# Gate and up products of a feed-forward layer: a second Strassen level for one of seven products, and a first tile whose loads are issued by need

## Chip, core and metric

One core of a Trainium2 chip runs the whole program. The metric is the device time in microseconds (us) of one execution; lower is better. The engines named below are TensorE (PE, with PEld for its weight loads), VectorE (DVE), ScalarE (ACT), GpSimd (POOL) and SyncE (SP), whose queue issues most of the DMAs.

## What is computed

One step of a hybrid layer over 1024 prompt rows and 32 sample rows of width 1024, all in fp32. An input projection feeds two groups of heads, attention and a recurrent mixing; their outputs are concatenated, projected and added to the input. The last part, where most of the change lies, is the feed-forward layer:

```
def layer_tail(x, attn, rw, attn_out_g, w_out, norm_ffn_g, w_gate, w_up, w_down):
    mix = jnp.concatenate([rmsnorm(attn, attn_out_g), rw], axis=-1)
    h = x + mix @ w_out
    u = rmsnorm(h, norm_ffn_g)
    return h + (jax.nn.silu(u @ w_gate) * (u @ w_up)) @ w_down
```

`w_gate` and `w_up` are 1024 x 2816, `w_down` is 2816 x 1024, and `u` has 1056 rows.

## The kernel before

The program has three stages. `layer_inputs` (L265 on) runs the input projection and the recurrence over nine tiles of 128 rows; `prompt_attention` follows, and `tail` (L2422 on) does the output projection and the feed-forward layer. Every engine has its own list of instructions in the order in which it is written; they meet at semaphores, so the order of the work is the written one.

**First tile of `layer_inputs`.** SP issues, in this order, the first tile `xt[0]`, the constants `gmix` and `con`, three of the six pieces of `w_in` (slots `wsl[0..2]`, 1472 KB each), a fourth piece in `area`, the second tile `xt[1]`, the vectors `vec`, and, after two pieces are done (`p_ok` 2), three smaller weights (L371 to L377). POOL waits for the constants, squares `xt[0]` and then multiplies it by `gmix` (L1526, L1528). PE makes six pieces; for pieces 4 and 5 ACT reloads slots 0 and 1 on its own DMA queue as soon as it has copied out the piece that used the slot, and slot 2 for the next tile (L1230).

**Gate and up in `tail`.** With FH = 11, KH = 4 and NW = 264, a *unit* is one pair of output blocks of 128 columns of `w_gate` or `w_up` (22 units), and each unit has two *steps*, one for each half `nh` of the columns of `u` (44 steps). A step is one level of Strassen-Winograd: seven products in place of eight, each of KH = 4 matmuls of 128x128 by 128x264, in four PSUM banks X, Y, Z, W. PE's order in a step is X = A11 B11 (copied out by ACT as `p1_`), Y = S2 T2, Z = S3 B12, W = S1 T1, then the three that close a bank: X += A12 B21, Z += A22 T4, W += S4 B22. `S1..S4` are sums of weight blocks that POOL makes for each unit (L2809 to L2814), `T1, T2, T4` sums of `u` that DVE makes once. DVE makes `u2 = Y + p1` (L2924), `u3 = Z + u2` (L2926) and `u3 = W + u3` (L2928); PE waits for the second before it closes Z and for the third before it closes W, and for `p1` before it closes X. Steps alternate between two sets of four banks, so that DVE and ACT have the next step's time to scale (by `rb`), gate (`th`, a tanh) and store in `hid`. The weights have two buffers `wA`, one for gate and one for up; a unit's two halves of 512 KB are loaded when the unit that used the buffer last is done.

**Down.** Eight steps of seven products of 11 matmuls on `hid`, with sums of `w_down` by POOL and of `hid` by DVE.

## Time and profile before

| what | value |
|---|---|
| three runs | 1798.8, 1803.51 and 1803.69 us, median 1803.51 |
| the profiled execution, its own time | 1797.16 us |
| its span (first to last instruction) | 1795.4 us |
| PE busy | 1725.1 us, 96% of the span |
| DVE, ACT, POOL busy | 950.4, 413.8 and 616.9 us |
| mean granted TensorE clock | 0.994 |

The profiled execution is one run of the same program with a recorder on. Its own time is 1.8 us above its span and 6.35 us below the median of the three runs, so sums of durations from the trace are made against 1797.16 and then set against the median. fp32 matmuls appear as two records each.

### The profile page before, as it was taken

Reading aid. Unit: us, or ns where it says so; the run is one execution under the profiler, and the core shown is the slowest. Engines: PE = TensorE matmul, PEld = TensorE weight load, DVE = VectorE, ACT = ScalarE, POOL = GpSimd, SP = SyncE. Lnnn points to the kernel's source line nnn. Section 1 sums busy time; section 2 is a strip of 40 time slices with the busy share of each in tenths; the row PEclk is TensorE's granted clock in tenths of the full one; section 3 lists DMA queues with packets and bytes.
Section 4 is the critical chain, followed back from the end, with each engine's and each line's share of the span. In section 5 each row is a group of like instructions: output and inputs, shape, how many; then the busy total and the mean of one; then the engine's idle time right before and its main releaser. Section 6 shows DMA issues by size and latency. Waiting matters only on the chain.

```text
span 1795.4 us, 34819 instructions
## 1 busy us (share of the span) xinstructions
PE 1725.1 (96%) x14732; PEld 1307.8 (73%) x14732; DVE 950.4 (53%) x1759; ACT 413.8 (23%) x945; POOL 616.9 (34%) x431
## 2 busy tenths in 40 slices
PE   5999999999998996999999999999999999999999
PEld 3566666666665664666667888888888888888887
DVE  2857767767767675666436433444434444526322
ACT  2343343343334232555212100011110010000000
POOL 2654653663653552001150221222212221635432
PEclk9999999999999998999999999999999999999999
DMA  8443253243244312620152111011110112333431
GB/s 349 166 154 105 69 166 109 66 159 109 80 134 115 107 38 73 185 60 1 34 208 97 47 48 47 24 47 47 48 48 24 48 47 77 121 105 105 145 96 62
DMA packets 89008, 169.36 MB, mean 94 GB/s; under 512 B 29627, under 2 KB 62987, under 8 KB 84630
## 3 DMA queue, kind: packets, MB, share of 16 engines
q1 hardware_dynamic: 80326, 119.16, 20.8%
q10 hardware_dynamic: 8528, 47.98, 7.7%
q8 instruction: 118, 1.93, 0.4%
q14 instruction: 36, 0.29, 0.0%
HBM read 136.40 MB, written 23.04 MB: 89 GB/s over the span
## 4 chain that ended last, share of the span: by engine, by line
PE 49%; DVE 1%; issue 0%; POOL 0%; ACT 0%; DVEq 0%
PE psum L2627 45%; PE psum L2580 4%; DVE u_sum L2890 0%; DVE mixT L2891 0%; PE psum L2615 0%; POOL row_ms L2804 0%; DVE mixT L2864 0%; DVE hid L2861 0%; DVE rb L2910 0%; PE psum L2621 0%; DVE hid L2851 0%; DVE part L2960 0%; DVE part L2924 0%; DVE yout L3018 0%; DVE part L2926 0%
## 5 line engine op out<-in xcount | busy, mean ns | idle before, releaser
L2627 PE MATMUL psum<-mixT,wA 128*128 128x264 f32 x1408 | 335.2, 386 | 0.4 <-DVE mixT L2891 0.4
L2627 PEld LDWEIGHTS psum<-mixT,wA 128*128 128x128 f32 x1408 | 267.4, 190 | 46.4 <-issue 0.8
L2627 PE MATMUL psum<-u_sum,wA 128*128 128x264 f32 x1232 | 297.2, 386 | 2.3 <-DVE part L2926 1.5
L518 PE MATMUL psum<-wsl,xt 128*128 128x368 f32 (+2 forms) x1100 | 287.7, 452 | 9.4 <-DMA wsl<-in_w_in 6.1
L2627 PEld LDWEIGHTS psum<-u_sum,wA 128*128 128x128 f32 x1232 | 233.8, 190 | 43.0 <-issue 3.2
L518 PEld LDWEIGHTS psum<-wsl,xt 128*128 128x128 f32 (+1 forms) x1100 | 151.9, 172 | 93.8 <-issue 20.0
L2809 POOL TENSOR_TENSOR wA<-wA 128x512 f32<-128x512 f32 x22 | 29.5, 1342 | 392.5 <-DMA wA<-in_w_gate 197.0
L2627 PE MATMUL psum<-hid,wA 128*128 128x264 f32 x528 | 120.2, 386 | 2.1 <-DVE hid L2962 1.5
L2627 PEld LDWEIGHTS psum<-hid,wA 128*128 128x128 f32 x528 | 100.2, 190 | 19.9 <-issue 2.8
L2213 PE MATMUL psum<-kT,qT 104*128 104x346 f32 (+7 forms) x224 | 78.3, 468 | 11.7 <-DMA kT<-scratch_kT 8.3
L1551 POOL TENSOR_TENSOR Ls<-Lraw,con 128x512 f32<-128x512 f32 x45 | 48.7, 1090 | 94.6 <-ACT Lraw L1165 66.1
L2627 PE MATMUL psum<-mixT,u_sum 128*128 128x264 f32 x352 | 79.8, 386 | 0.0
L2771 ACT ACTIVATE p<-psum 128x264 f32<-128x264 f32 x44 | 17.1, 390 | 253.6 <-PE psum L2627 253.4
L2627 PEld LDWEIGHTS psum<-mixT,u_sum 128*128 128x128 f32 x352 | 66.8, 190 | 11.7 <-POOL u_sum L2829 0.4
L1517 POOL TENSOR_TENSOR st<-st,con 128x3 f32<-128x3 f32 (+1 forms) x18 | 50.7, 2815 | 60.7 <-DVE st L1714 31.3
L1165 ACT ACTIVATE proj<-psum,rstd 128x368 f32<-128x368 f32 (+1 forms) x72 | 36.9, 512 | 143.4 <-PE psum L518 142.8
L2301 ACT ACTIVATE pq<-psum,neg 128x346 f32<-128x346 f32 (+7 forms) x112 | 59.8, 542 | 27.1 <-DVE neg L2382 20.9
L2379 DVE TENSOR_REDUCE part<-psum 128x1 f32<-128x347 f32 (+5 forms) x88 | 44.3, 524 | 40.6 <-PE psum L2213 39.5
L2819 POOL TENSOR_TENSOR wA<-wA 128x1408 f32<-128x1408 f32 x8 | 25.3, 3164 | 109.1 <-DMA wA<-in_w_down 109.1
L2790 ACT ACTIVATE p<-psum 128x264 f32<-128x264 f32 x8 | 3.1, 391 | 255.1 <-PE psum L2627 255.1
L2924 DVE TENSOR_TENSOR part<-psum,p 128x264 f32<-128x264 f32 x44 | 19.0, 433 | 79.1 <-PE psum L2627 79.0
L2353 POOL COPY wide<-rec 128x256 f32<-128x256 f32 x16 | 6.4, 400 | 152.0 <-DVE rec L2392 152.0
(367 smaller groups left out, 2898.2 us busy)
## 6 DMA issues: line engine op xcount, KB each, us to landing
wsl<-in_w_in ACTq DMA_DIRECT2D x27, 1472.0 KB, 6.5
wA<-in_w_down SPq DMA_DIRECT2D x32, 704.0 KB, 4.1
wA<-in_w_gate SPq DMA_DIRECT2D x22, 512.0 KB, 4.3
wA<-in_w_up SPq DMA_DIRECT2D x22, 512.0 KB, 4.3
mixed<-proj SPq DMA_DIRECT2D x8, 784.0 KB
...
wsl<-in_w_in SPq DMA_DIRECT2D x3, 1472.0 KB, 13.9
...
```

What stands on the lines that cost most here:

```text
L518: return pe.matmul(out, lhsT, rhs, start=start, stop=stop)
L1165: copy = lambda out, in_, **k: act.activation(out, in_, ACT.Copy, **k)
L1517: tt(out, ms, c_("minus_half")[:, 0:n], ALU.pow).then_inc(s[ok], 1)
L1551: tt(Ls[i % 2][:, :, :], Lraw[:, :, :], bcast(c_("levels")[:, i * 64:(i + 1) * 64], 1, H), ALU.mult).then_inc(s["Ls_ok"], 1)
L2213: pe.matmul(pb[n % BANKS][:, 0:y - x], qT[b][0:ROWS, t * P:(t + 1) * P], kT[b][0:ROWS, x:y], start=True, stop=True).then_inc(s["s_ps"], 1)
L2301: act.activation(rows_of(a, t)[:, x:y], pb[n % BANKS][:, 0:y - x], ACT.Exp, bias=neg[:, i % RINGS:i % RINGS + 1], accum_out=sums[:, pair % ...
L2379: dve.tensor_reduce(part[:, r, u:u + 1], src, AX.X, ALU.max).then_inc(s["part_ok"], 1)
L2580: last = pe.matmul(pb[bank][:, 0:c.stop - c.start], w[:, k, :], g.mixT[:, first_k + k, c], start=start and k == 0, stop=stop and k == 3, s ...
L2627: ins = pe.matmul(pb[bank][:, 0:NW], left(k), right(k), start=first and k == 0, stop=k == depth - 1, skip_group_check=not first)
L2809: tt(S1, A21, A22, ALU.add).then_inc(s["s1_ok"], 1)
L2819: tt(Ahi[:, 0:FH], Alo[:, 0:FH], Ahi[:, 0:FH], ALU.subtract).then_inc(s["e3_ok"], 1)
L2924: named(tt(u2, Y, p1_[it % 2][:, :], ALU.add), "y_done", it + 1)
```

## The change

In the first tile `xt[0]` is squared without a wait for the constants (the multiplication by `gmix` still waits for them), `vec` and the smaller weights are issued only when two pieces are done and slot 0 is reloaded, and slot 2 is reloaded later, after `lora_in(0)`.

In gate and up two units form a *double* (11 doubles: one that mixes gate and up, then five times two gate units and two up units). The product A12 B21 is left out of the four ordinary steps of a double, whose closing of X is gone with it; `p1_` has five buffers, so that the four X products stay. A fifth step makes the four A12 B21 blocks of the double together by a second Strassen level, with DK = 2 matmuls for each of seven products, from the sums `d1..d4` (POOL, for each double) and `t1, t2, t4` (DVE, once). DVE folds the kept products into it. A double of gate stores these corner blocks unscaled and they are scaled and gated in the first step of the next double (`scale_corner`, `gate_corner`). The load of A12 is a DMA of its own, after the fifth step. Down starts with blocks 0 to 3 and 10, then the rest.

```
+        sp.wait_ge(s["p_ok"], 2)
+        sp.wait_ge(s["w_sl0"], 32)
         sp.dma_start(vec[:, 0:MIX_END], io.vec[0:MIX_END].partition_broadcast(P)).then_inc(s["v_loaded"], 16)
-        sp.wait_ge(s["p_ok"], 2)
...
-            if n < SLOTS:
+            if n < SLOTS - 1:
...
         lora_in(0)
+        act.dma_start(wsl[2][:, :, :], io.w_in[SECOND[2]]).then_inc(s["w_sl2"], 16)
...
+            if p == 0:
+                pool.wait_ge(s["con_in"], 32)
             tt(xt[b][:, :, :], xt[b][:, :, :], bcast(gmix[:, :], 2, P), ALU.mult).then_inc(s["x_scaled"], 1)
...
-        pool.wait_ge(s["con_in"], 32)
...
+    DK = KH // 2
+    A12_ = [w[:, 0, KH:] for w in ab]
+    a11, a12 = A12_[0][:, 0:DK], A12_[0][:, DK:]
+    a21, a22 = A12_[1][:, 0:DK], A12_[1][:, DK:]
+    by_block = lambda x, n: x.rearrange("p (k n) -> p k n", n=n)
+    d1, d2 = (by_block(con[:, spare_b + i * DK * P:spare_b + (i + 1) * DK * P], P) for i in range(2))
+    d4 = by_block(g.spare[:, 3 * DK * NW:3 * DK * NW + DK * P], P)
+    b11, b12, b21, b22 = (B21u[:, DK * a:DK * a + DK, NW * c:NW * c + NW] for a in range(2) for c in range(2))
+    t1, t2, t4 = g.spare[:, 0:DK * NW], g.spare[:, DK * NW:2 * DK * NW], g.spare[:, 2 * DK * NW:3 * DK * NW]
+    t1, t2, t4 = (by_block(x, NW) for x in (t1, t2, t4))
...
+    DOUBLES = [((0, FH - 1), (1, FH - 1))] + [((b, p), (b, p + 1)) for p in range(0, FH - 1, 2) for b in range(2)]
+    STEPS = [(d, j) for d in range(FH) for j in range(5)]
+    N_STEPS = len(STEPS)
+    MIXED, GATES, UPS = 0, 1, 2
+
+    def double_kind(d):
+        return MIXED if d == 0 else GATES if DOUBLES[d][0][0] == 0 else UPS
...
+            (kind, pair), b = DOUBLES[u // 2][u % 2], u % 2
+            w = io.w_up if kind else io.w_gate
+            sp.dma_start(ab[b][:, 0, 0:KH], w[pair][:, 0:KH]).then_inc(s[f"w_in{b}"], 16)
+            sp.dma_start(ab[b][:, 1], w[pair + FH]).then_inc(s[f"w_in{b}"], 16)
+
+        def load_twelve(u):
+            (kind, pair), b = DOUBLES[u // 2][u % 2], u % 2
+            w = io.w_up if kind else io.w_gate
+            sp.dma_start(ab[b][:, 0, KH:], w[pair][:, KH:]).then_inc(s[f"w12_in{b}"], 16)
...
-        for u in range(2, UNITS):
-            sp.wait_ge(s["w_ps"], 2 * u - 2)
-            load_unit(u)
+        for d in range(1, FH):
+            sp.wait_ge(s["w_ps"], 5 * d - 3)
+            load_unit(2 * d)
+            sp.wait_ge(s["w_ps"], 5 * d - 1)
+            load_unit(2 * d + 1)
+            sp.wait_ge(s["w_ps"], 5 * d)
+            load_twelve(2 * d)
+            load_twelve(2 * d + 1)
...
-                pe.wait_ge(s["p1_ok"], it + 1)
-                product(X, left(A12), half(B21u), KH, "x_ps", first=False)
...
+            pe.wait_ge(s["u3_ok"], it + 1)
+            product(Z, left(A22), half(T4u), KH, "z_ps", first=False)
+            pe.wait_ge(s["s4_ok"], u + 1)
+            pe.wait_ge(s["c22_ok"], it + 1)
+            product(W, left(sw[b][:, 2]), half(B22u), KH, "w_ps", first=False)
...
+        def second_level(it, d):
+            X, Y, Z, W = (4 * (it % 2) + i for i in range(4))
+            pe.wait_ge(s["p1_ok"], it - 1)
+            for b in range(2):
+                pe.wait_ge(s[f"w12_in{b}"], 16 * (d + 1))
+            product(X, left(a11), left(b11), DK, "p1_ps")
+            pe.wait_ge(s["d2_ok"], d + 1)
+            pe.wait_ge(s["dt4_ok"], 1)
+            pe.wait_ge(s["y_done"], it - 1)
+            product(Y, left(d2), left(t2), DK, "p6_ps")
+            pe.wait_ge(s["d3_ok"], d + 1)
+            pe.wait_ge(s["z_done"], it - 1)
+            product(Z, left(a21), left(b12), DK, "p7_ps")
+            pe.wait_ge(s["d1_ok"], d + 1)
+            pe.wait_ge(s["w_done"], it - 1)
+            product(W, left(d1), left(t1), DK, "p5_ps")
+            pe.wait_ge(s["p1_ok"], it + 1)
+            product(X, left(a12), left(b21), DK, "x_ps", first=False)
+            pe.wait_ge(s["u3_ok"], it + 1)
+            product(Z, left(a22), left(t4), DK, "z_ps", first=False)
+            pe.wait_ge(s["d4_ok"], d + 1)
+            pe.wait_ge(s["c22_ok"], it + 1)
+            product(W, left(d4), left(b22), DK, "w_ps", first=False)
+
+        for it, (d, j) in enumerate(STEPS):
+            if j < 4:
+                first_level(it, d, j)
+            else:
+                second_level(it, d)
...
+                order = [0, 1, 2, 3, 10, 4, 5, 6, 7, 8, 9]
+                for k in order:
+                    if k == 4:
+                        pe.wait_ge(s["a11_in"], 16)
+                    elif k == 8:
+                        pe.wait_ge(s["hid_ok"], 16 * FH)
...
+        def fourth_sum(u):
+            b = u % 2
+            pool.wait_ge(s[f"w12_in{b}"], 16 * (u // 2 + 1))
             pool.wait_ge(s["s2_ok"], u + 1)
-            tt(S4, A12, S2, ALU.subtract).then_inc(s["s4_ok"], 1)
...
+                three_sums(2 * d)
+                three_sums(2 * d + 1)
+                fourth_sum(2 * d)
+                fourth_sum(2 * d + 1)
+            pool.wait_ge(s["w_ps"], 5 * d + 1)
+            pool.wait_ge(s["s4_ok"], 2 * d + 2)
+            tt(d1, a21, a22, ALU.add).then_inc(s["d1_ok"], 1)
+            pool.wait_ge(s["d1_ok"], d + 1)
+            tt(d2, d1, a11, ALU.subtract).then_inc(s["d2_ok"], 1)
+            tt(a21, a11, a21, ALU.subtract).then_inc(s["d3_ok"], 1)
+            pool.wait_ge(s["d2_ok"], d + 1)
+            tt(d4, a12, d2, ALU.subtract).then_inc(s["d4_ok"], 1)
...
+        def second_sums():
+            dve.wait_ge(s["t4_ok"], 1)
+            named(tt(t1, b12, b11, ALU.subtract), "dt1_ok", 1)
+            named(tt(t2, b22, t1, ALU.subtract), "dt2_ok", 1)
+            tt(b12, b22, b12, ALU.subtract).then_inc(s["dt3_ok"], 1)
+            tt(t4, b21, t2, ALU.subtract).then_inc(s["dt4_ok"], 1)
...
+                if double_kind(d) == UPS and j == 0:
+                    scale_corner(d)
...
+        def second_level(it, d):
...
+            front(it, X, Y, Z, W, p1_[4])
+            if kind == GATES:
+                tt(odd1, u3, p1_[3], ALU.add).then_inc(s["fold_ok"], 1)
+                dve.wait_ge(s["x_ps"], d + 1)
+                tt(even0, X, p1_[0], ALU.add).then_inc(s["x_done"], 1)
+                dve.wait_ge(s["z_ps"], it + 1)
+                named(tt(c21, Z, u2, ALU.add), "z_done", it + 1)
+                tt(odd0, c21, p1_[2], ALU.add).then_inc(s["fold_ok"], 1)
+                dve.wait_ge(s["w_ps"], it + 1)
+                named(tt(u2, W, u2, ALU.add), "w_done", it + 1)
+                named(tt(even1, u2, p1_[1], ALU.add), "fold_ok", 3 * d + 3)
+                return
...
+            named(tt(u3, u3, p1_[3], ALU.add), "fold_ok", 3 * d + 1)
+            if kind == UPS:
+                stt(odd1, odd1, 0.5, u3, ALU.mult, ALU.mult).then_inc(s["hid_ok"], 1)
+            dve.wait_ge(s["x_ps"], d + 1)
+            named(tt(g11[:, :], X, p1_[0], ALU.add), "x_done", d + 1)
+            if kind == UPS:
+                stt(even0, even0, 0.5, g11[:, :], ALU.mult, ALU.mult).then_inc(s["hid_ok"], 1)
+            else:
+                n_c11 += 1
+                named(tt(g11[:, :], g11[:, :], r0, ALU.mult), "c11_ok", n_c11)
+            dve.wait_ge(s["z_ps"], it + 1)
+            named(tt(c21, Z, u2, ALU.add), "z_done", it + 1)
+            named(tt(c21, c21, p1_[2], ALU.add), "fold_ok", 3 * d + 2)
+            if kind == UPS:
+                stt(odd0, odd0, 0.5, c21, ALU.mult, ALU.mult).then_inc(s["hid_ok"], 1)
+            dve.wait_ge(s["w_ps"], it + 1)
+            named(tt(u2, W, u2, ALU.add), "w_done", it + 1)
+            named(tt(u2, u2, p1_[1], ALU.add), "fold_ok", 3 * d + 3)
+            if kind == UPS:
+                stt(even1, even1, 0.5, u2, ALU.mult, ALU.mult).then_inc(s["hid_ok"], 1)
...
+        def scale_corner(d):
+            for i, h11 in enumerate(corner(d)):
+                tt(h11, h11, rb[:, i % 2 * NW:i % 2 * NW + NW], ALU.mult).then_inc(s["cs_ok"], 1)
...
```

PE's instructions of gate and up, in the middle of the stage (`mixT` holds u, `u_sum` its sums, `wA` the weights and their sums, `wo` and `con` the places of the new sums). Before, one step from the second product on, with the next step's first:

```order
L2627 MATMUL psum<-u_sum,wA 128x264 x4
L2627 MATMUL psum<-mixT,wA 128x264 x4
L2627 MATMUL psum<-u_sum,wA 128x264 x4
L2627 MATMUL psum<-mixT,wA 128x264 x4
L2627 MATMUL psum<-u_sum,wA 128x264 x4
L2627 MATMUL psum<-mixT,wA 128x264 x8
```

With the change, the last ordinary step of the first double and its fifth step:

```order
L2669 MATMUL psum<-mixT,wA 128x264 x8
L2669 MATMUL psum<-u_sum,wA 128x264 x4
L2669 MATMUL psum<-mixT,wA 128x264 x4
L2669 MATMUL psum<-u_sum,wA 128x264 x8
L2669 MATMUL psum<-mixT,wA 128x264 x6
L2669 MATMUL psum<-wo,con 128x264 x2
L2669 MATMUL psum<-mixT,wA 128x264 x2
L2669 MATMUL psum<-wo,con 128x264 x2
L2669 MATMUL psum<-mixT,wA 128x264 x2
L2669 MATMUL psum<-wo,wA 128x264 x2
L2669 MATMUL psum<-mixT,wo 128x264 x2
```

The four `mixT,wA` matmuls between W = S1 T1 and the closing of Z are gone, so these two stand together as `u_sum,wA` x8, and each double ends with 14 matmuls in pairs.

SP's queue in the first tile, before:

```order
L373 DMA xt<-in_x_tiles 128x1024
L374 DMA vec<-in_vec 128x2368
L377 DMA wkv<-in_w_kv_up 128x1024 [waits p_ok]
L377 DMA wq<-in_w_q_up 128x1536
L377 DMA w2a<-in_w2a 128x512
```

With the change:

```order
L373 DMA xt<-in_x_tiles 128x1024
L376 DMA vec<-in_vec 128x2368 [waits w_sl0,p_ok]
L378 DMA wkv<-in_w_kv_up 128x1024
L378 DMA wq<-in_w_q_up 128x1536
L378 DMA w2a<-in_w2a 128x512
```

`vec` no longer follows `xt` at once; everything behind it in the queue has moved with it.

DVE's instructions of the fifth step of a double of up, with the first of the next double (only the change has it; `p_0`, `p_1` and `con` are the kept X products):

```order
L3051 TENSOR_TENSOR part<-psum,part 128x264
L3112 TENSOR_TENSOR part<-part,con 128x264
L3114 SCALAR_TENSOR_TENSOR hid<-hid,part 128x264
L3116 TENSOR_TENSOR g<-psum,p_0 128x264
L3118 SCALAR_TENSOR_TENSOR hid<-hid,g 128x264
L3123 TENSOR_TENSOR part<-psum,part 128x264
L3124 TENSOR_TENSOR part<-part,con 128x264
L3126 SCALAR_TENSOR_TENSOR hid<-hid,part 128x264
L3128 TENSOR_TENSOR part<-psum,part 128x264
L3129 TENSOR_TENSOR part<-part,p_1 128x264
L3131 SCALAR_TENSOR_TENSOR hid<-hid,part 128x264
L3047 TENSOR_TENSOR part<-psum,p_0 128x264
```

Seven of these rows (L3112, L3114, L3118, L3124, L3126, L3129, L3131) read tiles in SBUF and nothing in PSUM; before, a step of up had three such instructions (L2954, L2961, L2962).

## Rows read from the trace of the kernel before

**Rows 1.** The page, busy time of PE, weight loads, DVE, ACT, POOL

```profile
PE 1725.1 (96%) x14732; PEld 1307.8 (73%) x14732; DVE 950.4 (53%) x1759; ACT 413.8 (23%) x945; POOL 616.9 (34%) x431
```

**Rows 2.** Waits of PE over the whole span: total, times, longest (us)

```profile
PE psum L518 <- DVE xs L1686: 13.6, 1, 13.6
...
PE psum L518 <- DMA wsl<-in_w_in: 6.1, 2, 5.1
```

**Rows 3.** Waits of PE from 955 to 1520 us, gate and up

```profile
PE psum L2627 <- DVE part L2926: 1.5, 1, 1.5
PE psum L2627 <- DVE hid L2962: 1.5, 1, 1.5
```

**Rows 4.** Timeline of the first tile: start, duration, engine, instruction, idle before it

```profile
9.53 1.89 POOL L1526 TENSOR_TENSOR xsq<-xt 128x1024 f32<-128x1024 f32 x1 [6.81 <-DMA con<-in_con]
...
14.23 9.31 PE L518 MATMUL psum<-wsl,xt 128*32 128x184 f32 x192 [0.36 <-DVE mean_sq L1707]
...
20.02 0.39 ACTq L1230 DMA_DIRECT2D wsl<-in_w_in  x1
...
23.72 2.70 PE L518 MATMUL psum<-area,xt 128*32 128x184 f32 x64 [0.19 <-DMA area<-in_w_in]
...
31.57 4.19 PE L518 MATMUL psum<-wsl,xt 128*32 128x184 f32 x64 [5.15 <-DMA wsl<-in_w_in]
...
36.69 2.70 PE L518 MATMUL psum<-wsl,xt 128*32 128x184 f32 x64 [0.94 <-DMA wsl<-in_w_in]
...
47.49 1.88 PE L518 MATMUL psum<-wkv,area 128*128 128x512 f32 x4
```

**Rows 5.** DMA issues at 2.1, 2.6 and 3.6 us: median us to landing

```profile
wsl<-in_w_in SPq DMA_DIRECT2D x1, 1472.0 KB, 10.8
...
wsl<-in_w_in SPq DMA_DIRECT2D x2, 1472.0 KB, 12.4
...
area<-in_w_in SPq DMA_DIRECT2D x1, 1472.0 KB, 20.0
```

**Rows 6.** The DMA issue of ACT at 20.0 us: us to landing

```profile
wsl<-in_w_in ACTq DMA_DIRECT2D x1, 1472.0 KB, 11.4
```

**Rows 7.** DMA queues, 0 to 26 us, SP's and ACT's: packets, MB, share

```profile
q1 hardware_dynamic: 1253, 8.92, 86.4%
q10 hardware_dynamic: 48, 0.57, 5.4%
```

**Rows 8.** Timeline of one step of up, 1493.8 to 1506.3 us

```profile
1493.79 1.94 PE L2627 MATMUL psum<-mixT,wA 128*128 128x264 f32 x8
...
1495.84 0.43 DVE L2926 TENSOR_TENSOR part<-psum,part 128x264 f32<-128x264 f32 x1 [1.32 <-PE psum L2627]
1497.35 1.94 PE L2627 MATMUL psum<-mixT,wA 128*128 128x264 f32 x8
1497.62 0.43 DVE L2928 TENSOR_TENSOR part<-psum,part 128x264 f32<-128x264 f32 x1 [1.35 <-PE psum L2627]
...
1506.25 1.94 PE L2627 MATMUL psum<-mixT,wA 128*128 128x264 f32 x8
```

**Rows 9.** Timeline of the first step of gate and up

```profile
966.36 3.80 PE L2627 MATMUL psum<-mixT,wA 128*128 128x264 f32 x16 [0.37 <-DVE mixT L2891]
...
971.09 0.43 DVE L2926 TENSOR_TENSOR part<-psum,part 128x264 f32<-128x264 f32 x1
...
971.67 2.02 PE L2627 MATMUL psum<-u_sum,wA 128*128 128x264 f32 x8 [1.51 <-DVE part L2926]
```

**Rows 10.** Instructions on wA and of L2954: ns min/median/max, first and last start

```profile
L2814 POOL TENSOR_TENSOR wA<-wA x22: 1262/1462/2290, 924.4 to 1474.2; 128x512 f32<-128x512 f32 x22
...
L2954 DVE SCALAR_TENSOR_TENSOR hid<-hid,part x22: 432/434/1512, 999.7 to 1510.5; 128x264 f32<-128x264 f32 x22
```

**Rows 11.** DMA of the weights on tile wA: us to landing

```profile
DMA to landing us min/median/max: 3.3/4.2/12.9
```

**Rows 12.** Timeline, start of down: first sum of POOL, and its last

```profile
1515.34 0.33 SPq L2544 DMA_DIRECT2D wA<-in_w_down  x1
...
1519.79 3.16 POOL L2819 TENSOR_TENSOR wA<-wA 128x1408 f32<-128x1408 f32 x1 [44.14 <-DMA wA<-in_w_down]
...
1534.77 2.57 POOL L2829 TENSOR_TENSOR u_sum<-u_sum,wA 128x128 f32<-128x128 f32 x1
```

385 lines of the change are left out of this document (225 added, 160 removed).

## Prediction

> **What bounds the kernel now.** I read the page first: PE is busy 1725.1 us, 96% of the span [rows 1], so time is won by fewer matmuls or by fewer waits of PE. The list of PE's waits then says where it is not busy: 13.6 us at the very start, and 6.1 us in the first tile for reloaded pieces of `w_in` [rows 2]. In gate and up it waits almost nowhere: 1.5 us once in the first step, for `u3`, and 1.5 us once at the end, for `hid` [rows 3]. Third, the timeline of one step there: the same product starts at 1493.79 and at 1506.25, so a step is 12.46 us [rows 8], which is 12.46/28 = 0.445 us for each of its 28 matmuls, 1.78 us for a product of four. There a matmul removed is 0.445 us gained, as long as nothing that it covered comes out.
>
> **Gate and up: the matmuls.** Before, 44 steps x 28 = 1232. With the change each double has 4 x 24 + 14 = 110, 11 doubles 1210. 22 fewer x 0.445 = **-9.8 us**.
>
> **What the removed product covered.** In a step PE waited for `u3 = Z + u2` only after the product A12 B21. In [rows 8] Z ends at 1495.57, W = S1 T1 fills PE to 1497.35, A12 B21 to 1499.13. DVE's L2926 starts at 1495.84 and is done at 1496.27; L2928 is done at 1498.05. The closing of Z moves from 1499.13 to 1497.35, that of W from 1500.91 to 1499.13: both margins fall from 2.86 to 1.08 us, and stay positive. DVE can be 1.08 us late at no cost. In the fifth step a product takes 0.89 us: `u3` is due 2 x 0.89 after Y's successor starts, and DVE's instruction after Z ends costs 0.27 + 0.43 = 0.70 us, so it is done 0.19 us before W ends and 1.08 us before Z is closed.
>
> The first step is the exception. There W is made early, and after Z only A12 B21 stood before the closing of Z: PE was busy from 966.36 for both, waited 1.51 us for L2926 (which started at 971.09, held by DVE's own list: sums of `u`, squares) and went on at 971.67 [rows 9]. DVE's list ahead of this is unchanged, so the closing still starts at 971.67. The 1.78 us of the removed product turn into wait: **+1.8 us**. The wait there should read about 3.3 us.
>
> **The seams between doubles.** Counted from the end of a double's fifth step (14 x 0.445 = 6.23 us long): the loads for the second unit are issued at -6.2, land 4.2 us later [rows 11], after two issues, and let POOL do three sums from about -1.4 to 2.4 (about 1.27 us each). A12 is issued at 0, lands near 4.5, and the fourth sum of the first unit is done near 6. It is due when W is closed, after five products, at 8.9: 2.9 us of slack. While POOL sums, DVE folds. An instruction of DVE on SBUF alone takes 0.43 us, but 1.51 when POOL is summing; POOL's sum takes 1.26 us, but its median in L2814 is 1.46 and its maximum 2.29 [rows 10]. Seven such instructions stand in the fifth step of a double of up. With free ports they end 1.9 us after the step. If each of POOL's first three sums and one of the fourth ones blocks one of them for 1.1 us, they end at 6.3, `u2` of the next step at 6.7 and `u3` at 7.2, where it is due at 7.12: about nothing is lost. The doubles of gate fold with three such instructions and are clear. For ten seams I take **+0.5 us**; bounds 0 and, at 0.5 us each, 5.
>
> The Trainium skill bears on this (SBUF — State Buffer, section "SBUF: two separate sides"): the port pair of VectorE and GpSimd is an exclusive lock, held for the whole instruction, which a VectorE operation with two SBUF inputs needs too. The trace agrees, with 1.51 us against 0.43. By that rule alone every one of the seven could be blocked in full, 7 x 1.1 = 7.7 us, and `u3` would be 3.4 us late in five seams, 17 us in all.
>
> That bound is not reached, since POOL has five sums in this window and can block one instruction with each; 5 x 1.1 would make `u3` about 1.2 us late, in five seams 6 us. POOL's four corner sums (half as wide, about 0.65 us) run early in the second step and are due in the fifth, over 30 us later. `second_sums` on DVE is 4 instructions of 528 elements, at 0.43 us for 264 about 0.85 each at most, 3.4 us; PE's third step asks for `u3` 7.1 us after it starts, DVE is free 5.5 us after, no cost. `scale_corner` and `gate_corner` fill DVE's idle time in a step (it waits 1.3 us per product).
>
> **The start of down** keeps its length. PE no longer waits 1.5 us for `hid` (blocks 8 and 9 come last), but waits for the load of blocks 4 to 7 after five matmuls: issued at the end, at least 3.3 us to land [rows 11], against 2.2 us of matmuls, 1.2 us or more. POOL's sums decide there: in before they start 4.45 us after the last load's issue and run to 1537.3 [rows 12]; the load that starts them is now issued second, 0.4 us later, but is smaller. 0, bounds -1.5 and +1.5.
>
> Gate, up and this seam together: -9.8 + 1.8 + 0.5 = **-7.5 us**, bounds -9.8 and -1.
>
> **The first tile** is bound by loads. With a start at 2.1 and 10.8 us to landing, slot 0 is there at 12.9; the middle of the next two, 12.4, makes slot 1 land at 16.6; `area` is there at 3.6 + 20.0 = 23.6 [rows 5]. So squaring `xt` without the constants moves PE's first piece only from 14.23 to 12.9, and the fourth still starts at 23.6, as before [rows 4]. The gain is behind it. ACT's reload of slot 0 was issued at 20.0 and took 11.4 us [rows 6], to 31.4; PE had ended the fourth piece at 26.42 and idled 5.15 us. Up to 26 us ACT's queue had moved 0.57 MB and SP's 8.92 [rows 7]; up to and including `xt[1]` SP had 7.96 MB to move (512 + 4 + 860 + 4 x 1472 + 512 KB), so 0.96 MB of `vec` went ahead. With `vec` held, the reload is issued at 18.8 (the first piece ends 1.3 us sooner), and the two queues must move 7.96 + 1.51 = 9.47 MB. Both moved 9.49 MB by 26 us; landing trails the bytes (`area` is the last of 7.44 MB, which at the mean of 0.365 MB/us are through at 20.4, and landed at 23.6; the rate was lower at first, so 2 us is my choice out of 2 to 3). So slot 0 lands near 28.0, 3.4 us sooner, and slot 1, 1.51 MB more at about 400 GB/s, near 31.5.
>
> PE then makes the fifth piece from 28.0. It took 4.19 us after the long idle time and 2.70 otherwise [rows 4]; after 1.6 us of idling it lies between, and I keep 4.19, to 32.2. The last piece ends at 34.9 where it ended at 39.39: **-4.5 us**. Bounds: all DMA waits gone and the fast rate, -7.8; nothing but half of the 1.3 us at the front, -0.7. The held loads are `vec` and 1536 KB: 2.8 MB behind 1.5 MB of slot 1 from 30 us on, at 400 GB/s until about 39; PE wants the last at 47.49 - 4.5 = 43.0 [rows 4]. Behind SP's new wait stand also the row of `state_shift` and the copies of `mixed`, small and wanted later than that; ACT's moved issue stands behind `lora_in(0)`, where ACT idles, and its slot is wanted some 10 us later. If the held loads came 8 us later than this they would cost what they bring.
>
> The Trainium skill (DMA: Bandwidth & Descriptors, section "Queues, rings and completion order") says that a DMA engine takes turns between the queues for which it has work. ACT's 0.57 MB in about 4 us against SP's, 143 of 400 GB/s, is a share of a third rather than of half. By turns of equal weight the reload would take bandwidth from `area` and the fourth piece would be up to 1 us later, with the reload sooner by as much.
>
> **Sum.** -7.5 - 4.5 = -12.0 us: the profiled execution at 1785.2 instead of 1797.16, the median, 6.35 above it, at **1791.5 us**. A difference below 0.3% (5.4 us) is what a measurement of this kernel can't tell from none.
>
> **Rivals.**
> *Only gate and up pay* (0.14): what is held back comes too late or the reload is no sooner, because it is bound by its own queue. For it: it got a third of the bandwidth while others were served. Against: 5.15 us of waiting behind 0.95 MB of a transfer that nobody wanted yet. -7.5 - 0.7: 1795.3.
> *Only the first tile pays* (0.14): the ports cost the bound worked out above, 6 us over five seams, and POOL's sums 0.1 to 0.2 late at all ten. For it: 1.51 and 2.29 us in [rows 10], margins down to 1.08. Against: no wait inside before. -1.5 - 4.5: 1797.5.
> *Slower* (0.05): the late A12. The loads of `wA` took up to 12.9 us to land [rows 11]; the fourth sum has 2.9 us of slack, and beyond a landing of 4.2 + 2.9 = 7.1 us each further us costs one at each of ten seams. At 9 us to landing it is +19 us, 1810; it decides from about 8.8 us on. Against: 12.9 was at the start, with other loads under way; the median is 4.2.
> *More* (0.07): the first tile's bound of -7.8 and no loss at a seam: -15.8, 1787.7, or down to 1783.
> The forecast (0.60) spans 1787 to 1796 by itself.
>
> The range reaches from the best case, 1784, to 1799. Faster by over 0.3% is below 1798.1: the forecast, *more*, most of *only gate and up* and half of *only the first tile*, less the spread of 4.9 us between runs: 0.82. Within: 0.13. Slower: 0.05.
>
> **What would show it.** In gate and up: ordinary steps of 24 x 0.445 = 10.68 us and fifth steps of 6.23; one wait of 3.3 us in the first step; waits for L3049 (`u3`), L3051 or POOL's fourth sum elsewhere would be the seams. In the first tile: the wait of 5.15 us down to about 1.6, the last piece ended near 35, and PE's first `wkv` product near 43 rather than 47.5. I am wrong if seams show more than 0.5 us, or if the first `wkv` product waits for a DMA.

## The result and the profile after

| | before | changed |
|---|---|---|
| median of four runs | 1803.6 us (1798.8 to 1804.16) | 1788.16 us (1787.9 to 1789.94) |
| profiled execution, its own time | 1797.16 us | 1789.94 us |
| span | 1795.4 us | 1788.3 us |
| PE busy | 1725.1 us | 1718.5 us |

The ratio is 0.9922, with a 95% interval of 0.9908 to 0.9936: 14.1 us of 1803.6 by the ratio, 15.4 by the medians, and inside the range given. The profiled pair differs by 7.2 us only. How much of the 14 us belongs to the change is the main question of what follows.

The page's first part (busy time, share of the span, instructions) answers to [rows 1]:

```profile
PE 1718.5 (96%) x14688; PEld 1301.1 (73%) x14688; DVE 1022.4 (57%) x1862; ACT 416.0 (23%) x956; POOL 655.6 (37%) x475
```

The 22 matmuls fewer are 44 records. DVE has 72 us more work and POOL 39, so the seams are the place to look. PE's waits over the whole span answer to [rows 2] and [rows 3]:

```profile
PE psum L519 <- DVE xs L1689: 8.5, 1, 8.5
PE psum L519 <- DMA wsl<-in_w_in: 5.3, 3, 2.8
...
PE psum L2669 <- DVE part L3049: 3.9, 2, 3.3
...
PE psum L2669 <- POOL u_sum L2950: 1.5, 1, 1.5
...
PE psum L519 <- DMA area<-in_w_in: 1.2, 1, 1.2
...
PE psum L2778 <- DMA wA<-in_w_down: 0.7, 1, 0.7
```

**First tile.** PE's timeline, against [rows 4]:

```profile
8.54 0.28 PE L519 MATMUL psum<-con,xs 128*32 128x1 f32 x8 [8.54 <-DVE xs L1689]
...
11.57 9.91 PE L519 MATMUL psum<-wsl,xt 128*32 128x184 f32 x192 [2.75 <-DMA wsl<-in_w_in]
...
17.96 0.39 ACTq L1231 DMA_DIRECT2D wsl<-in_w_in  x1
...
22.67 2.70 PE L519 MATMUL psum<-area,xt 128*32 128x184 f32 x64 [1.19 <-DMA area<-in_w_in]
...
26.93 2.70 PE L519 MATMUL psum<-wsl,xt 128*32 128x184 f32 x64 [1.56 <-DMA wsl<-in_w_in]
...
30.58 2.70 PE L519 MATMUL psum<-wsl,xt 128*32 128x184 f32 x64 [0.95 <-DMA wsl<-in_w_in]
...
41.58 1.88 PE L519 MATMUL psum<-wkv,area 128*128 128x512 f32 x4
```

The reload of slot 0, issued at 17.96, and the load of `area`, issued at 3.55, as the list of DMA issues has them (KB, us to landing), against [rows 5, 6]:

```profile
wsl<-in_w_in ACTq DMA_DIRECT2D x1, 1472.0 KB, 8.8
...
area<-in_w_in SPq DMA_DIRECT2D x1, 1472.0 KB, 19.0
```

The wait of 5.15 us is 1.56, the last piece ends at 33.28 where it ended at 39.39, and the first `wkv` product starts at 41.58 instead of 47.49: 5.9 us gained, with no DMA wait ahead of it.

**The first step of gate and up**, against [rows 9]:

```profile
956.42 1.94 PE L2669 MATMUL psum<-mixT,wA 128*128 128x264 f32 x8
...
963.09 2.02 PE L2669 MATMUL psum<-mixT,wA 128*128 128x264 f32 x8 [0.38 <-DVE mixT L3012]
968.40 3.70 PE L2669 MATMUL psum<-u_sum,wA 128*128 128x264 f32 x8 [3.29 <-DVE part L3049]
```

The wait reads 3.29 us where 3.3 was forecast. What was not forecast stands beside it: the product behind it took 3.70 us, not 2.02. The window over it shows why (busy time of PE, PEld, DVE, ACT, POOL, then the granted clock):

```profile
968.40:971.40 3.00, 3.00 (x7) 2.38 (x8) 1.57 (x2) 0.11 (x1) 0.00 (x0) 0.51 0.11 45
```

The clock was at 0.51, the lower level of 1.2 GHz, through these 3 us.

The step behind it also lost time. PE's and DVE's rows there, and then the same place in the kernel before, where the removed product stood between the two that now follow each other (986.49 to 988.27):

```profile
983.13 4.08 PE L2669 MATMUL psum<-u_sum,wA 128*128 128x264 f32 x16
...
984.67 0.43 DVE L3049 TENSOR_TENSOR part<-psum,part 128x264 f32<-128x264 f32 x1
...
987.04 3.72 PE L2669 MATMUL psum<-mixT,wA 128*128 128x264 f32 x16
```

```profile
984.71 1.94 PE L2627 MATMUL psum<-u_sum,wA 128*128 128x264 f32 x8
...
988.27 1.94 PE L2627 MATMUL psum<-u_sum,wA 128*128 128x264 f32 x8
```

W = S1 T1 starts at 983.13 and is through at 984.91, but `u3` is done only at 985.10, since DVE comes late from the copy of `rb` (L3031). The two products take 3.91 us where 2 x 1.78 = 3.56 would do: 0.35 us lost, which the removed product had covered before. The list of waits does not show it, because it merges the two products into one row.

**The seams.** Behind the first, mixed double stands the only wait of PE in the ten seams that the view lists. Timeline:

```profile
1014.64 1.40 POOL L2902 TENSOR_TENSOR wA<-wA 128x512 f32<-128x512 f32 x1 [17.18 <-DMA wA<-in_w_gate]
...
1015.42 0.92 DVE L3121 TENSOR_TENSOR g<-g,rb 128x264 f32<-128x264 f32 x1
...
1017.43 1.46 POOL L2905 TENSOR_TENSOR wA<-wA 128x512 f32<-128x512 f32 x1
...
1018.25 0.92 DVE L3129 TENSOR_TENSOR part<-part,p 128x264 f32<-128x264 f32 x1
...
1019.17 2.68 POOL L2911 TENSOR_TENSOR wA<-wA 128x512 f32<-128x512 f32 x2 [0.29 <-DMA wA<-in_w_gate]
1019.21 1.53 DVE L3134 TENSOR_TENSOR part<-part,rb 128x264 f32<-128x264 f32 x1
...
1020.77 1.39 DVE L3136 SCALAR_TENSOR_TENSOR hid<-yout,g 128x264 f32<-128x264 f32 x1
...
1024.30 2.05 PE L2669 MATMUL psum<-u_sum,wA 128*128 128x264 f32 x8 [0.60 <-DVE part L3049]
```

DVE's instructions on SBUF alone take 0.92 to 1.53 us while POOL sums (0.43 alone), and PE waits 0.60 us for `u3`. Each of the five stretched instructions of the seam ends 0.2 to 0.3 us after the end of the POOL sum that it met: the one of 1015.42 at 1016.34, the sum at 1016.04; the one of 1018.25 at 1019.17, the sum at 1018.89. A seam behind a double of up just holds:

```profile
1113.72 1.38 DVE L3114 SCALAR_TENSOR_TENSOR hid<-hid,part 128x264 f32<-128x264 f32 x1
...
1115.18 1.94 PE L2669 MATMUL psum<-mixT,wA 128*128 128x264 f32 x8
...
1118.06 2.90 POOL L2911 TENSOR_TENSOR wA<-wA 128x512 f32<-128x512 f32 x2 [0.41 <-DMA wA<-in_w_gate]
...
1118.78 1.04 DVE L3129 TENSOR_TENSOR part<-part,p 128x264 f32<-128x264 f32 x1
1119.85 1.39 DVE L3131 SCALAR_TENSOR_TENSOR hid<-hid,part 128x264 f32<-128x264 f32 x1
...
1121.75 0.43 DVE L3049 TENSOR_TENSOR part<-psum,part 128x264 f32<-128x264 f32 x1
```

The step starts at 1115.18, `u3` is done 7.00 us later and due 4 x 1.78 = 7.12 us later. POOL's fourth sums, both in the row of 2.90 us, are done at 1120.96 and due at 1115.18 + 5 x 1.78 = 1124.1, 3.1 us of slack where 2.9 was forecast: the late A12, the rival on the slow side, never came near. The doubles behind the first are 48.95 to 49.0 us long, and 110 x 0.445 is 48.95, except the second (49.82) and the sixth (49.24). Over the ten that is 1.3 us more than counted; in the other seven traces with the new feed-forward layer it is 1.0 to 1.7 us, with 0.8 to 1.3 of it in the second double each time.

**The start of down**, against [rows 12]:

```profile
1507.20 2.39 PE L2778 MATMUL psum<-hid,wA 128*128 128x264 f32 x10
...
1509.57 3.18 DVE L3184 TENSOR_TENSOR hid<-hid 128x2904 f32<-128x2904 f32 x1
1510.24 2.94 PE L2778 MATMUL psum<-hid,wA 128*128 128x264 f32 x12 [0.66 <-DMA wA<-in_w_down]
1510.98 4.79 POOL L2940 TENSOR_TENSOR wA<-wA 128x1408 f32<-128x1408 f32 x1 [38.55 <-DMA wA<-in_w_down]
...
1530.20 2.05 PE L2669 MATMUL psum<-mixT,u_sum 128*128 128x264 f32 x8 [1.52 <-POOL u_sum L2950]
```

The wait for `hid` is gone, but PE now waits 1.52 us for POOL, whose first sum took 4.79 us where it took 3.16. It began inside a long instruction of DVE (L3184, which ends at 1512.75) and is done 3.02 us after that one's end. Before, DVE's instruction had begun 3.1 us ahead of the sum (1516.70 against 1519.79) and was nearly through. From the end of gate and up to this product it was 22.0 us before and is 23.0 now.

### The profile page after: what moved, and what is told of

The parts are those of the page before. It is cut to its first block, busy times and chain, and to the rows that moved or that the text cites. A ratio compares the mean times of both kernels' runs of the same rounds, so it can differ in the third digit from the quotient of the medians.

```text
span 1788.3 us, 35061 instructions
## 1 busy us (share of the span) xinstructions
PE 1718.5 (96%) x14688; PEld 1301.1 (73%) x14688; DVE 1022.4 (57%) x1862; ACT 416.0 (23%) x956; POOL 655.6 (37%) x475
## 4 chain that ended last, share of the span: by engine, by line
PE 43%; issue 3%; POOL 2%; SPq 1%; DVE 1%; DMA 1%; DVEq 0%; POOLq 0%
PE psum L2669 43%; DMA wA<-in_w_gate 1%; POOL u_sum L2945 0%; POOL u_sum L2949 0%; POOL wA L2940 0%; POOL wA L2902 0%; SPq L2514 0%; SPq L2515 0%; POOL wA L2911 0%; DMA wA<-in_w_down 0%; SPq L2517 0%; POOL u_sum L2950 0%; POOL wA L2904 0%; SPq L2520 0%; POOL row_ms L2920 0%
## 5 line engine op out<-in xcount | busy, mean ns | idle before, releaser
L2669 PE MATMUL psum<-u_sum,wA 128*128 128x264 f32 x1232 | 292.8, 388 | 4.8 <-DVE part L3049 3.9
L2669 PE MATMUL psum<-mixT,wA 128*128 128x264 f32 x1188 | 284.4, 386 | 0.4 <-DVE mixT L3012 0.4
L2669 PEld LDWEIGHTS psum<-mixT,wA 128*128 128x128 f32 x1188 | 225.7, 190 | 39.4 <-issue 0.8
L2669 PE MATMUL psum<-hid,wA 128*128 128x264 f32 x506 | 115.1, 386 | 0.6 <-ACT p L2886 0.6
L2669 PEld LDWEIGHTS psum<-hid,wA 128*128 128x128 f32 x506 | 96.1, 190 | 17.3 <-issue 1.0
L2846 ACT ACTIVATE yout<-part 128x264 f32<-128x264 f32 x67 | 28.3, 423 | 195.0 <-DVE part L3066 133.2
L2886 ACT ACTIVATE p<-psum 128x264 f32<-128x264 f32 x8 | 3.1, 390 | 250.5 <-PE psum L2669 239.7
L2216 PEld LDWEIGHTS psum<-kT,qT 104*128 104x128 f32 x224 | 38.3, 194 | 27.7 <-issue 18.7
```

The costliest lines, as they stand in the source:

```text
L2216: pe.matmul(pb[n % BANKS][:, 0:y - x], qT[b][0:ROWS, t * P:(t + 1) * P], kT[b][0:ROWS, x:y], start=True, stop=True).then_inc(s["s_ps"], 1)
L2669: ins = pe.matmul(pb[bank][:, 0:NW], left(k), right(k), start=first and k == 0, stop=k == depth - 1, skip_group_check=not first)
L2846: halved = lambda out, in_: act.activation(out, in_, ACT.Tanh, scale=0.5)
```

## Experiments

All are variants of the two kernels, timed beside the kernel before in three series (b_again to squares_later; after_again to con_only; hold_both to squares_third), each series on a chip of its own. In them the kernel before had medians of 1800.99 (29 runs), 1798.91 (12) and 1800.77 us (15). Three numbers from each trace tell more than the medians: the start of the first `wkv` product (what the first tile did), the length of the way from the first product of gate and up to the first of down (what that stage did), and the length of attention and output projection, from the first `kT` product to the first of gate and up, in which PE's instructions are the same in every kernel here. Each of the three comes from one profiled execution. In us:

| kernel | first `wkv` | `kT` start | attention to gate and up | gate and up | median (number of runs) | ratio [95%] |
|---|---|---|---|---|---|---|
| before | 47.49 | 713.02 | 246.67 | 557.12 | 1803.6 (4) | 1 |
| changed | 41.58 | 708.89 | 247.53 | 550.78 | 1788.16 (4) | 0.9922 [0.9908, 0.9936] |
| b_again | 46.36 | 712.94 | 247.55 | 557.12 | 1803.0 (12) | 1.0007 [0.9995, 1.0018] |
| tile_only | 41.76 | 707.84 | 250.89 | 557.12 | 1795.93 (12) | 0.9973 [0.9963, 0.9983] |
| ffn_only | 47.56 | 715.94 | 250.88 | 549.50 | 1795.83 (12) | 0.9972 [0.9959, 0.9985] |
| squares_later | 41.51 | 707.33 | 246.67 | 548.98 | 1788.22 (5) | 0.9936 [0.9921, 0.995] |
| after_again | 41.43 | 709.70 | 250.89 | 548.94 | 1791.64 (7) | 0.9963 [0.9949, 0.9976] |
| squares_again | 41.88 | 708.91 | 247.48 | 548.31 | 1789.98 (6) | 0.9948 [0.9934, 0.9962] |
| vec_only | 45.21 | 715.25 | 250.92 | 557.12 | 1803.56 (1) | |
| con_only | 47.32 | 713.27 | 249.38 | 557.12 | 1800.05 (1) | |
| hold_both | 42.53 | 708.89 | 250.91 | 557.12 | 1798.51 (11) | 0.9988 [0.9977, 0.9999] |
| fill_first | 41.82 | 707.31 | 250.88 | 549.41 | 1790.36 (5) | 0.994 [0.9928, 0.9953] |
| after_third | 45.56 | 711.74 | 249.41 | 552.07 | 1793.73 (5) | 0.9949 [0.9935, 0.9963] |
| squares_third | 41.50 | 709.36 | 248.37 | 550.73 | 1792.18 (5) | 0.9947 [0.9935, 0.996] |

### The kernel before again, as the yardstick

No edit.

> The kernel before, unchanged, run again with a new profile. Its runs so far lie at 1797.2, 1798.8 and 1803.5 to 1804.2 us. Theory A (the executions differ by where PE's clock drops or a DMA lands late in the first 100 us or at the start of attention): times again in both groups, ratio 1.000 within 0.003, and the profile shows which stretch is longer. Theory B (the runs above 1803 are the kernel's own time, and the profiled execution of 1797 was a lucky one): nearly all at 1803 to 1804.

1.0007: one program against itself. Its single runs lie in two groups, five from 1797.27 to 1799.7 and seven from 1802.59 to 1804.42, so theory A held: executions of one program differ. Its first `wkv` product is at 46.36, 1.1 us sooner than in [rows 4].

### Each part alone

tile_only keeps the first tile's lines of the change and the feed-forward layer of before; ffn_only the reverse. Both as edits of the changed kernel, shortened:

```
 # tile_only: layer_inputs as changed, the whole of tail as before
-    DOUBLES = [((0, FH - 1), (1, FH - 1))] + ...
...
-        for d in range(1, FH):
...
+        for u in range(2, UNITS):
+            sp.wait_ge(s["w_ps"], 2 * u - 2)
+            load_unit(u)
...
 # ffn_only: tail as changed, in layer_inputs
+        sp.dma_start(vec[:, 0:MIX_END], ...)
         sp.wait_ge(s["p_ok"], 2)
-        sp.wait_ge(s["w_sl0"], 32)
-        sp.dma_start(vec[:, 0:MIX_END], ...)
...
-            if n < SLOTS - 1:
+            if n < SLOTS:
...
-        act.dma_start(wsl[2][:, :, :], io.w_in[SECOND[2]]).then_inc(s["w_sl2"], 16)
...
-            if p == 0:
-                pool.wait_ge(s["con_in"], 32)
...
+        pool.wait_ge(s["con_in"], 32)
```

> The kernel before with the edits of the first tile alone. Additive theory: the first wkv product of PE starts near 41.6 us instead of 47.5 (5.9 us), of which some 3 to 6 are left at the end: time 4 to 6 us below before. Rival, that attention's own waits take it back (the start of gate and up moved by only 3.3 us in the changed kernel): 2 to 3 us below before. Second rival, that the change of 14 us in the medians sits in this part: over 8 us below.

> The changed kernel with the loads, waits and order of the first tile put back as before; second Strassen level in gate and up stays. Additive theory: from the start of gate and up to the second sum of down's first step 574 us against 578 before, time 4 to 8 us below before. Rival, that this part brings the larger share of the 14 us: 9 us or more below before.

0.9973 and 0.9972 of 1801 us, 4.9 and 5.0 us: both parts pay, about equally, and together 10 us. Both additive theories held. In the traces each part moves its own column of the table, the first `wkv` product (41.76 against 47.49) or gate and up (549.50 against 557.12). The second is 7.6 us shorter, of which 1.5 us is the wait for `hid`; with the start of down, where PE now waits for a load and for POOL, 5.1 us are left (572.5 against 577.6).

### The first tile, edit by edit

```
 # vec_only: the kernel before, but
+        sp.wait_ge(s["p_ok"], 2)
+        sp.wait_ge(s["w_sl0"], 32)
         sp.dma_start(vec[:, 0:MIX_END], ...)
-        sp.wait_ge(s["p_ok"], 2)
 # con_only: the kernel before, but
+            if p == 0:
+                pool.wait_ge(s["con_in"], 32)
...
-        pool.wait_ge(s["con_in"], 32)
 # hold_both: vec_only, and
-            if n < SLOTS:
+            if n < SLOTS - 1:
...
+        act.dma_start(wsl[2][:, :, :], io.w_in[SECOND[2]]).then_inc(s["w_sl2"], 16)
```

> The kernel before with only the issue of the vectors held until two pieces are done and slot 0 is reloaded. Theory, that the vectors in SP's queue hold back both the reload and, as they follow closely, the loads ahead of them: con lands 6.3 us after its issue instead of 7.8, slot 0 near 11.5 instead of 12.9, its reload about 9 us after issue instead of 11.4, the first wkv product near 42.5. Rival, that only the reload gains: con and slot 0 as before, the wkv product near 44.

> The kernel before with only the wait for the constants moved behind the squaring of the first tile. Theory, that slot 0 of w_in bounds the first piece: PE's first piece starts at 12.9 instead of 14.2, with the wait on the load, and the fourth piece (area) at 23.6 to 25 as before, so that the first wkv product moves by at most 1.3 us. Rival: the earlier first piece brings the reload forward in full and the wkv product moves by 1.3 us or more.

> The kernel before, with two of the three edits of the first tile: the vectors and smaller weights held back, and slot 2 reloaded after lora_in(0), but not the squaring ahead of the constants. Theory (slot 2's reload is what made the held weights late in vec_only): PE waits for no DMA before its first wkv product, the wait of 2.43 us for w2a is gone, the fifth piece waits about 2.1 us as in vec_only, the last piece starts at about 31.4 us and the first wkv product at about 42.5 to 43.5 (45.21 in vec_only, 47.49 in the kernel before, 41.76 in tile_only). Rival A (the held weights are late because they are issued at 21 us, whatever ACT's queue does): the wait of over 2 us stays and the first wkv product is at 45. Rival B (the constants edit carries half): first wkv product later than 44. Time: 2.5 to 5 us below the kernel before, ratio 0.9973 to 0.999, or within the spread of no change by rival A.

con_only only moves the wait: PE is ready at 9.36 and waits 3.32 us for slot 0, then 4.88 us for the same reload. Its first `wkv` product is 0.2 us sooner than in [rows 4], as its theory had it. PE's timeline of con_only:

```profile
12.97 10.26 PE L518 MATMUL psum<-wsl,xt 128*32 128x184 f32 x192 [3.32 <-DMA wsl<-in_w_in]
...
31.22 4.69 PE L518 MATMUL psum<-wsl,xt 128*32 128x184 f32 x64 [4.88 <-DMA wsl<-in_w_in]
```

vec_only has the sooner reload (8.3 us to landing where it took 11.4), but its first `wkv` product comes at 45.21: the theory (42.5) and the rival (44) both missed. It waits for the held weights, which now share the bandwidth with slot 2's reload. PE's timeline of vec_only:

```profile
27.87 2.70 PE L519 MATMUL psum<-wsl,xt 128*32 128x184 f32 x64 [2.08 <-DMA wsl<-in_w_in]
...
45.21 1.98 PE L519 MATMUL psum<-wkv,area 128*128 128x512 f32 x4 [2.43 <-DMA w2a<-in_w2a]
```

The same place in hold_both, where slot 2's reload is held too, has no wait:

```profile
42.53 1.02 PE L519 MATMUL psum<-wkv,area 128*128 128x512 f32 x2
```

So of the 5.9 us, holding `vec` brings 2.3 alone (47.49 to 45.21) and with slot 2 held 5.0 (42.53); squaring ahead of the constants adds 0.8 (41.76 in tile_only). The expected 42.5 to 43.5 held, and the rivals fell. These parts come from one execution each, and b_again stands 1.1 us from the kernel before, so the 0.8 is not clear of chance. By its median hold_both is only 2.3 us below the kernel before, less than its 5 us at `wkv`, at nearly the same mean clock of the runs (0.9905 and 0.9909); where the rest of its lead goes is not shown.

### The first step: the clock, and a way to shorten the wait

```
 # squares_later (also squares_again, squares_third): DVE, the changed kernel, but
-        add_squares(KD - 2)
...
             front(it, X, Y, Z, W, p1_[j])
             if it == 0:
+                add_squares(KD - 2)
                 row_means()
 # fill_first: PE, the changed kernel, but in the first step, after W and Z
             if it == 0:
+                pe.wait_ge(s["p1_ok"], 1)
+                product(X, left(A11), half(B12u), KH, "filler_ps")
                 pe.wait_ge(s["t4_ok"], 1)
```

fill_first makes one product more, A11 B12, in the bank X that ACT has copied out; its result is overwritten. after_again and after_third are the changed kernel.

> The changed kernel with DVE's next to last sum of squares put behind the three sums of the first gate step. Theory, that PE's wait of 3.3 us in this step lets its clock fall and costs 1.8 us beside the wait itself: the wait falls to about 2.0 us; if the clock then stays high the closing of Z takes 1.8 instead of 3.5 us and the time falls by 3.0 us. Rival, that a wait of 2.0 us is enough for the clock to fall, or that it depends on when it comes: the wait is 1.25 us shorter and the closing stays at 3.5: 1.3 us below the changed kernel.

> The changed kernel, unchanged, in one call with the others. Alone the first tile gave a ratio of 0.9973 and the second Strassen level 0.9972, together 10 us; both together had given 0.9922 or 14 us. Additive theory: a ratio near 0.9945 (10 us, within 0.15%), and the 14 us owed 4 us to which executions of before were drawn. Rival, that the parts help each other (fewer drops of the clock when both are in): 0.992 again.

> The changed kernel with the next to last sum of squares put behind the three sums of the first gate step, again, now beside the changed kernel. Theory: 1 us faster than it (1.25 us less wait in the first step, 0.4 given back before the row sums), no more, since whether the clock falls in this stretch is chance. Rival: 3 us faster, if the shorter wait spares the clock as a rule.

> The changed kernel a third time, beside the others of this call. Theory (both parts pay, and what differs between two executions of one program is the granted clock at idle places far from the change): ratio between 0.992 and 0.997, first wkv product at 41.5 to 42, stage of gate and up to the first product of down 549 to 551 us, against 557.1 before. Rival (a part of the gain was chance): ratio above 0.9975.

> The changed kernel with the squares of the last but one block put behind u3 in the first step, a third time beside the changed kernel. Theory: the wait in the first step is 2.0 us instead of 3.3, and 0.4 of the 1.3 us is given back at the row sums, so the way from the stage's first product to the first of down is about 0.6 us shorter than after_third's (548.3 to 549.0), and the median is 0.5 to 3 us below it. Rival (no gain that can be measured): the medians within 0.5 us of each other.

> The changed kernel with one product of four matmuls more in the first step of gate and up, made while PE would wait for u3 (it repeats the first product into the same bank, so the result stays what it was). It fills 1.78 us of the wait of 3.29 us. Theory (in the first step the removed product is only turned into a wait, and the fall of the granted clock behind it is by chance): the wait reads about 1.5 us, the closing of Z starts at the same distance of 15.0 us from the first product of the stage or up to 0.1 later, and the way from the stage's first product to the first product of down is 549 to 551 us as in the changed kernel without it. Rival (the wait of 3.29 us makes the clock fall): the way is 1.5 us shorter than in the profiled execution of the changed kernel, and never over 549.2. Time: the same as after_third within 1.5 us.

The 3.29 us wait stood in all four traces with it; the clock fell behind it in two (`changed`, `after_third`) and not in the other two. PE's timelines of after_again and of after_third:

```profile
972.56 2.02 PE L2669 MATMUL psum<-u_sum,wA 128*128 128x264 f32 x8 [3.29 <-DVE part L3049]
```

```profile
973.13 3.86 PE L2669 MATMUL psum<-u_sum,wA 128*128 128x264 f32 x8 [3.29 <-DVE part L3049]
976.78 3.07 PE L2669 MATMUL psum<-mixT,wA 128*128 128x264 f32 x8
```

The fall costs 1.7 us in `changed` (the product takes 3.54 us to the next one's start instead of 1.86) and about 3.0 in after_third (552.07 against 548.94 and 549.50). In the seven traces with 1.50 or 1.51 us of wait for the same operand (the six with the feed-forward layer of before, and fill_first) it never fell there. That speaks for the wait as the cause, but two falls in four are too few to call it shown. fill_first has the wait of 1.50 us and a way of 549.41, the same as the changed kernel without a fall: filling the wait neither costs nor brings time of its own. The closing of Z starts 11.97 us behind the stage's first product, 11.98 in `changed`; the 15.0 of the expectation was wrong. Its rival set a limit of 549.2, between the 548.94 and 549.50 of the changed kernel without a fall, so the 549.41 does not decide. Its median was to be within 1.5 us of after_third's and is 3.4 below (1790.36 against 1793.73).

With the squares behind `u3` the wait is 1.99 us, as expected. The row sums then give back 0.7 us, 0.43 of it as a wait, and the way is 0.6 us shorter (548.31 against 548.94). In two of the three traces the clock fell behind the row sums instead (a product of 3.66 in squares_later, of 3.89 in squares_third), so a shorter first wait did not spare the fall: there were two in three traces here and two in four without the edit. squares_third's way of 550.73 lies outside the 548.3 to 549.0 expected. squares_later was to be 1.3 or 3.0 us below the changed kernel, which was not timed in its series. Beside the changed kernel in the same series the edit's median is 1.7 and 1.6 us lower, between the 1 and the 3 us of squares_again's two theories (1789.98 against 1791.64, 1792.18 against 1793.73), but the intervals overlap (0.9948 and 0.9963; 0.9947 and 0.9949). It is the best version tried by a hair, and not shown to be faster.

after_again's ratio of 0.9963 lies just above the 0.993 to 0.996 of its additive theory, and its interval shuts out the rival's 0.992. after_third's ratio held, but its first `wkv` product (45.56 for 41.5 to 42) and its way (552.07 for 549 to 551) did not. It had a late start: slot 1's reload landed 12.0 us after its issue instead of 10.1, PE waited 2.88 us, and the last piece took 4.38 us instead of 2.70.

### Where 14, 7 and 9 us come from

The changed kernel came out at 0.9922, 0.9963 and 0.9949 of the kernel before, three intervals of which the first and second do not meet. The attention column shows differences of this size: it goes from 246.67 to 250.92 though PE's instructions there are the same, with and without the change. Windows of 5 us from the start of the first `kT` product, behind PE's wait for the load of `kT`, in the kernel before (246.67) and in con_only (249.38); the last three numbers are the granted clock, DMA share and GB/s:

```profile
713.00:718.00 5.00, 4.29 (x8) 2.51 (x8) 1.93 (x5) 0.33 (x1) 0.00 (x0) 0.57 0.38 102
718.00:723.00 5.00, 4.24 (x21) 3.03 (x22) 3.08 (x7) 3.82 (x15) 0.00 (x0) 1.00 0.89 222
```

```profile
713.30:718.30 5.00, 4.26 (x8) 2.46 (x8) 1.93 (x5) 0.38 (x1) 0.00 (x0) 0.50 0.24 69
718.30:723.30 5.00, 4.59 (x11) 3.07 (x12) 1.71 (x4) 1.69 (x8) 0.00 (x0) 0.50 1.00 261
```

In the second five microseconds PE made 21 instructions at the full clock and 11 at the half. In windows of 2 us the clock is back about 4 us behind the start of the first `kT` product in the kernel before, and 12 us behind it in con_only, tile_only and after_again: up to 8 us later, at a cost of 2.7 to 3.4 us. A second fall stands in the window of 10 us that starts 170 us behind the first `kT` product, in nine of the fourteen traces. In the kernel before, where it is missing, and in `changed`:

```profile
883.02:893.02 10.00, 8.52 (x40) 6.29 (x39) 6.46 (x11) 0.00 (x0) 1.64 (x1) 1.00 0.07 24
878.89:888.89 10.00, 9.07 (x35) 6.96 (x35) 6.07 (x9) 0.00 (x0) 1.61 (x1) 0.83 0.00 1
```

These two events sort the whole column: neither, 246.67; the fall alone, 247.48 to 247.55; the late return alone, 249.38 and 249.41; both, 250.88 to 250.92 (squares_third, 248.37, has its return in between). All four kinds stand on both sides of the change, so nothing here ties them to it. Summed with the falls in the first step (0, 1.7 or 3.0) and a start that can be 4 us later, one execution of the changed kernel differs from the next by several us.

The single runs say the same. Each has its mean granted clock on record. Over the kernel before's 29 runs of the first series the time falls as it rises: 1802.6 us on average at 0.988 and 0.989 (eight runs), 1796.1 at 0.994 (three). The four runs of the changed kernel that gave the 14 us had the high clock (0.993 to 0.996, mean 0.9943); those of after_again and after_third had 0.9906 and 0.9896. Over the 56 runs of the kernel before that were timed beside the variants and all 16 of the changed one, both mean clocks are at 0.991, and the mean times are 1800.05 and 1791.45. That gives 8.6 us as an estimate of the change's worth at equal clock, and makes about 5 of the 14 us a matter of which executions were drawn. What the chips themselves add is not shown, since the series differ in both.

## Why the prediction held, and where its terms were off

**Sum.** Forecast: -12.0 by the traces' own terms. Measured by the ratios: -14.1, -6.7 and -9.2 (by medians -15.4, -7.3 and -7.0), -9.9 as the sum of the two parts alone, and 8.6 us at equal clock. The size forecast was too large by some 3 us, and the first measurement, the largest of the three, owes part of its nearness to luck. So does the median of 1788.16, 3.3 us below the 1791.5 of the forecast: the profiled execution came out 4.7 us above its own 1785.2, and the 6.35 us added for the median, the distance in the kernel before, was -1.8 us in the changed one. In the profiled pair the lead was 5.9 us at the first `wkv` product, 4.1 at `kT`, 3.3 at the start of gate and up (the fall of the clock in attention) and 7.1 at the end. Inside the sum one term was too cautious (first tile, by 1.4) and one too hopeful (gate, up and the seam, by 1.8 to 3.7), and the two errors partly cancel.

**First tile, -4.5.** Measured -5.9 at the first `wkv` product, within the bounds. Two choices were cautious. The reload landed at 26.8, not 28.0: it was issued at 17.96 and not 18.8, since slot 0 itself landed 1.3 us sooner (PE's first piece starts at 11.57, not 12.9), and it took 8.8 us. And I kept 4.19 us for the fifth piece; it took 2.70, as in each of the other traces in which PE had waited 1.5 to 2.1 us there. It took 4.19 to 4.69 behind the waits of 2.83 us (b_again) to 5.15 in the kernels with the old order of loads; in the kernel before the granted clock reads 0.50 from 31.5 to 34.5. Of the 2.6 us so won by the end of the fifth piece, 0.95 went into the wait for slot 1. The fourth piece, which turns of equal weight between the queues would have put up to 1 us later, came sooner: `area` took 19.0 us to land and not 20.0. Slot 1's 16.6 was right, though the 12.4 of [rows 5] is the middle of slots 0 and 1 and not of the next two. That the held loads would not be late was right, but only because slot 2 was held too: vec_only priced that at 2.4 us. Not all of the gain arrives: tile_only brings 4.9 us, and in the profiled pair the lead is 4.1 at the `kT` product (713.02 against 708.89). What takes the rest between these two places is not shown.

**Matmuls, -9.8.** The count and the price were right: doubles of 48.95 us. "DVE can be 1.08 us late at no cost" was right too, but the second step of the stage was not looked at: there DVE is later than that, behind the copy of `rb`, and 0.35 us came out.

**First step, +1.8.** The wait was right to 0.01 us; the clock behind it was missing from the sum, 0 to 3 us.

**Seams, +0.5.** Measured 1.3 us in the profiled execution (0.87 in one seam, 0.29 in another, the rest in crumbs) and 1.0 to 1.7 in the others, so by the prediction's own sign, seams that show more than 0.5 us, this step was wrong. The seam of up was worked out as `u3` at 7.2, due at 7.12; it was 7.00. The one that lost most is the mixed double's, which I had not counted apart: it scales, gates and multiplies in its tail, so nine instructions on SBUF stand where a double of up has seven. The Trainium skill (SBUF — State Buffer, section "SBUF: two separate sides") describes an exclusive lock, held for the whole instruction. The trace agrees: instructions of DVE are stretched by 0.5 to 1.1 us and end just behind the POOL sum that they met. The bound of 17 us was not reached, since the five sums of a seam stretched five instructions, as the prediction assumed.

**Start of down, 0.** Measured +0.9. The step that failed is that POOL's chain keeps its length. It started 0.7 us sooner behind the end of gate and up (3.8 for 4.5), and its first sum took 1.6 us longer behind DVE's L3184.

Gate, up and this seam together were put at -7.5. From the first product to the second product on `mixT,u_sum` of down's first step it was 577.6 us before (1537.3 less 959.69) and 573.8 in the profiled execution, -3.8. ffn_only and after_again give 572.5 and 571.9, -5.1 and -5.7. The terms as measured close on it: -9.8 + 1.8 + 0.35 + the seams (1.3, 1.7 and 1.1 us in the profiled execution, ffn_only and after_again) + 0.9 is -5.45, -5.05 and -5.65, and the profiled one has 1.7 us of clock on top, -3.75. **The step that was mis-sized is this term**, by 1.8 to 2.4 us of work (seams 0.6 to 1.2, start of down 0.9, second step 0.35) and 0 to 3 us of clock.
